# Experts chosen for twelve tiles beside the last output products, a first stage in a new order, and x1 kept in the weight ring

## The reference, cut to what matters

```python
def reference(x, c, w_ada, b_ada, ...):
    cond = jax.nn.silu(c)
    ada = (cond @ w_ada[l] + b_ada[l])[:, None, :]
    sh1, sc1, g1, sh2, sc2, g2 = jnp.split(ada, 6, axis=-1)
    h = rms_norm(x, norm1_gain[l]) * (1.0 + sc1) + sh1
    mix, v_first = token_mixer(h, ...)        # h @ w_in, a short convolution, a recurrence by chunks, @ w_out
    x = x + g1 * mix
    h2 = rms_norm(x, norm2_gain[l]) * (1.0 + sc2) + sh2
    x = x + g2 * moe(h2, w_router, router_bias, w_expert_in[l], w_expert_out[l])
    return rms_norm(x, final_gain)

def moe(h, w_router, router_bias, w_e_in, w_e_out):
    aff = jax.nn.sigmoid(hf @ w_router)
    sel = (aff + router_bias).reshape(t, N_GROUPS, EXPERTS_PER_GROUP)
    gscore = jnp.sum(lax.top_k(sel, TOP_K)[0], axis=-1)     # best group of 8, then the top 2 of its 4 experts
    gsel = jnp.argmax(gscore, axis=-1)
    ...
    # rows sorted by expert, each expert padded to blocks of 128 rows
    yb = lax.map(expert_block, (buf.reshape(n_blocks, M_BLK, d), blk_e))
    ye = yb.reshape(n_rows, d)[dest] * wts...
    return jnp.zeros_like(hf).at[tok].add(ye)
```

## Time and profile before

| | us |
|---|---|
| three runs | 4644.1, 4650.66, 4652.82 (median 4650.66) |
| the profiled execution | 4651.68 |
| its span in the trace | 4649.9 |
| first stage | 152.7 |
| last output product to the list of rows (`IDX`) | 3361.6 to 3451.6, 90 |
| last stage | 4556.3 to 4649.9, 93.6 |
| busy: PE, DVE, ACT, POOL | 4245.8 (91%), 1599.6 (34%), 1310.1 (28%), 321.6 (7%) |

### The profile page before, as it was taken

One profiled execution on the slowest core, in us unless ns is written; L12 is line 12 of the kernel. 1 busy time (PEld: TensorE's weight loads), 2 busy tenths in 40 slices (PEclk: granted clock), 3 DMA queues, 4 the chain that ended last, 5 costly groups with the idle time before them and its releaser, 6 DMA issues.

```text
span 4649.9 us, 91708 instructions
## 1 busy us (share of the span) xinstructions
PE 4245.8 (91%) x36691; PEld 2256.6 (49%) x36691; DVE 1599.6 (34%) x3167; ACT 1310.1 (28%) x2960; POOL 321.6 (7%) x422
## 2 busy tenths in 40 slices
PE   6999999999999999999999999989949999999991
PEld 4455555555555555555555555555524444444440
DVE  3333433443334333434433443432241111111115
ACT  4123333333333333333333333333301111111115
POOL 0000100010001000000100010000000000000004
PEclk8999999999999999999999999999959999999995
DMA  8101000100100100100100100024349999999998
GB/s 313 52 8 36 23 11 22 36 9 16 41 13 9 48 8 13 46 11 8 50 11 8 40 19 11 6 83 151 112 161 411 411 411 411 411 411 411 411 411 328
DMA packets 251199, 628.36 MB, mean 135 GB/s; under 512 B 11602, under 2 KB 96820, under 8 KB 250804
## 3 DMA queue, kind: packets, MB, share of 16 engines
q1 hardware_dynamic: 232372, 555.52, 31.8%
q0 software_dynamic: 11520, 41.95, 2.3%
q10 hardware_dynamic: 6912, 25.17, 1.3%
HBM read 561.75 MB, written 60.84 MB: 134 GB/s over the span
## 4 chain that ended last, share of the span: by engine, by line
PE 86%; issue 5%; DVE 4%; DMA 2%; ACT 2%; SPq 1%; POOL 0%; DVEq 0%; POOLq 0%; ACTq 0%
PE bank L958 38%; PE bank L1295 9%; PE bank L1299 5%; PE bank L1172 5%; PE bank L1325 5%; PE duo L1083 4%; PE bank L1329 2%; PE duo L1072 2%; PE duo L1070 1%; DMA yb<-y_s,dix 1%; PE duo L1276 1%; ACT xs L1361 1%; PE bank L1015 1%; PE duo L895 1%; PE bank L999 1%
## 5 line engine op out<-in xcount | busy, mean ns | idle before, releaser
L958 PE MATMUL bank<-hT,w 128*128 (+1 forms) x4096 | 1790.3, 594 | 0.0
L958 PEld LDWEIGHTS bank<-hT,w 128*128 128x128 f32 x4096 | 777.1, 190 | 993.4 <-issue 993.4
L1295 PE MATMUL bank<-W,xT 128*128 128x512 f32 x1024 | 446.5, 594 | 2.2 <-DVE xT L2200 1.5
L1361 ACT ACT_TABLE_LOAD x268 | 343.8, 1283 | 21.0 <-DVE ub L1919 14.3
L1295 PEld LDWEIGHTS bank<-W,xT 128*128 128x128 f32 x1024 | 192.7, 191 | 233.3 <-issue 233.3
L2206 DVE TENSOR_TENSOR gsig<-bank,gsig 128x512 f32<-128x512 f32 x48 | 33.2, 692 | 672.8 <-ACT gsig L1361 672.8
L1299 PE MATMUL bank<-W,xT 128*64 128x512 f32 x1024 | 227.2, 598 | 18.0 <-issue 18.0
L723 POOL TENSOR_TENSOR Tm<-Tm,idents 128x512 f32<-128x512 f32 x32 | 40.5, 1265 | 2822.2 <-DVE Tm L1952 2822.2
L1172 PE MATMUL bank<-wo,mT 128*128 128x512 f32 x512 | 232.5, 600 | 0.0
L1325 PE MATMUL bank<-W,aT 128*128 128x512 f32 x512 | 225.1, 592 | 0.0
L1361 ACT ACTIVATE gsig<-bank 128x512 f32<-128x512 f32 x48 | 28.7, 597 | 657.8 <-PE bank L1295 423.3
(11 more groups left out here) (366 smaller groups left out, 5520.0 us busy)
## 6 DMA issues: line engine op xcount, KB each, us to landing
W<-in_w_expert_in_dram SPq DMA_DIRECT2D x128, 2048.0 KB, 25.5
W<-in_w_expert_out_dram SPq DMA_DIRECT2D x64, 2048.0 KB, 25.4
w<-in_w_in_dram SPq DMA_DIRECT2D x64, 512.0 KB, 3.9
adaw<-in_w_ada_dram SPq DMA_DIRECT2D x12, 2048.0 KB, 12.7
y_s<-ysb ACTq DMA_DIRECT2D x48, 512.0 KB, 6.7
xt<-in_x_dram SPq DMA_DIRECT2D x16, 512.0 KB, 9.1
WAc<-rank_s SPq DMA_DIRECT2D x32, 256.0 KB, 3.3
GDc<-rank_s SPq DMA_DIRECT2D x32, 256.0 KB, 3.3
```

The lines of the kernel that those rows point to most:

```text
L958: ins = mm(PJ[j % 2][:, :], w[:, j, k, :], hT[:, k, ds(group(i) * G, G)], start=k == 0, stop=k == KT - 1)
L1295: ins = mm(GU[half][:, :], xT[:, slot, kk_, :], ring_rows(parts[0])[:, k, cols], start=kk_ == 0, stop=kk_ == KT - 1)
L1361: return nc.scalar.activation(o, i, f, **kw)
```

## The change

It has three parts.

*First stage.* The four pieces of `rows2` are loaded first, by SP, and the fourteen pieces of `rows1` are loaded from ACT's queue; `cond` is made before the mask constants are finished. On all engines the order of a group becomes: `rank(g)`, then the transposes and evacuation of group g + 1, then two parts of `ada`. ACT evacuates group 0 before it takes the norm of group 1, and evacuates group g + 1 between its two halves of `rank`. On SP the save of group 0 and the loads of x group 3 and of parts 6 and 7 come before the eight column blocks, where the column blocks came before the first save.

*Choice of experts.* The chain is written as functions of a part: part 0 is tiles 0 to 11, part 1 tiles 12 to 15. Part 0 is worked through on DVE between the residuals and evacuations of the last four tiles, ACT takes its sigmoid then (`affinity(0)`), and PE its counts (`ranks(0)`). Part 1 follows after the last logits, on a quarter of the elements. The block table is compared on 128 partitions (one `tensor_scalar` and one reduction of 128 x 64) and turned into a row by two small products on PE (`M0`, `M1`). The step L2125 moves behind `blk`. The tiles of the stage are laid elsewhere in SBUF so that this may overlap.

*Last stage.* x1 is loaded as four pieces of 2 MB, each into a slot of `W1`, as soon as PE is through with that slot, while the last experts are computed; the buffer `x8` is gone. All gathers' indices are copied once. ACT takes root and exponent for two tiles at a time, and DVE writes the outputs of a pair after the additions of the next pair. The loops over tiles are written out.

```diff
+        pw = ExitStack()
+        W1 = sb(pw, "W1", [P, 4, KT * DE])
         p7 = ExitStack()
-        W1 = sb(p7, "W1", [P, 4, KT * DE])
...
+        X_SLOTS = (0, 1, 4, 5)
+
+        def x_rows8(n):
+
+            return W1[:, n // NF, n % NF * D:n % NF * D + D]
...
+            sp.dma_start(rows2[10:18, :], rows_of(io["c"])).then_inc(S["rows2_in"], 16)
+            sp.dma_start(rows2[0:8, :], rows_of(io["norm2_gain"])).then_inc(S["rows2_in"], 16)
+            sp.dma_start(rows2[8:10, :], mu[24:26, :]).then_inc(S["rows2_in"], 16)
+            sp.dma_start(rows2[18:66, :], rows_of(io["b_ada"])).then_inc(S["rows2_in"], 16)
...
-            load_x(3)
             load_ups(0)
             load_gate(0)
+            save_rank(0)
+            load_x(3)
+            for n in ADA_OF[1]:
+                load_ada(n)
+            sp.wait_ge(S["rank_saved"], 32)
+            sp.dma_start(WAc[:, :], rank_s[0, :, 0:G]).then_inc(S["wa_in"], 16)
+            sp.dma_start(GDc[:, :], rank_s[1, :, 0:G]).then_inc(S["gd_in"], 16)
             for j in range(8):
                 load_col(j, 0)
-            for g in range(NG):
+            for g in range(1, NG):
                 save_rank(g)
-                if g == 0:
-                    sp.wait_ge(S["rank_saved"], 32)
-                    sp.dma_start(WAc[:, :], rank_s[0, :, 0:G]).then_inc(S["wa_in"], 16)
-                    sp.dma_start(GDc[:, :], rank_s[1, :, 0:G]).then_inc(S["gd_in"], 16)
                 if g + 1 < NG:
                     for n in ADA_OF[g + 1]:
                         load_ada(n)
...
-            def load8(n, s):
-                if not new8(n):
-                    sp.wait_ge(S["x2_ready"], n - NF + 1)
-                sp.dma_start(x8[:, s], x1_s[ds(n * P, P), :]).then_inc(x_rows_in[s], 16)
+            def load8(g):
+                ring_free(NB // 6, X_SLOTS[g])
+                sp.dma_start(W1[:, g, :].rearrange("p (t d) -> p t d", d=D),
+                             x1_s[g * NF * P:(g + 1) * NF * P, :].rearrange("(t p) d -> p t d", p=P))\
+                    .then_inc(x_rows_in[g], 16)
...
-            for s in range(2):
-                sp.wait_ge(SL["y_out"][s], 16 * ((NBLK + 1 - s) // 2))
-            for s in range(NF):
-                load8(s, s)
-            with sp.Fori(1, NTILE // NF) as h:
...
+            for g in range(NTILE // NF):
+                load8(g)
+            for n in range(NTILE):
+                store8(n, n % NF)
...
             for g in range(NG):
+                rank(g)
                 if g + 1 < NG:
-                    if g:
-                        for n in ADA_OF[g - 1]:
-                            ada(n)
-                        for n in ADA_OF[g - 1]:
-                            ada_columns(n)
                     transpose_x(g + 1)
-                if g == NG - 1:
-                    for n in ADA_OF[2]:
-                        ada(n)
-                    for n in ADA_OF[2]:
-                        ada_columns(n)
-                rank(g)
-            for n in ADA_OF[3]:
-                ada(n)
-            for n in ADA_OF[3]:
-                ada_columns(n)
+                for n in ADA_OF[g]:
+                    ada(n)
+                for n in ADA_OF[g]:
+                    ada_columns(n)
             pe.wait_ge(S["ada_col"], 12)
             tr(SA[0:48, 0:P], adaT[:, :], ident[:, :]).then_inc(S["ada_T"], 1)
...
+            def ranks(part):
+                cols = tile_cols(part)
+                pe.wait_ge(S["rank_mm"], 2 * part + 1)
+                mm(PJ[0][:, cols], sut[:, :], lg[6][:, cols], start=True, stop=True)
+                mm(PJ[1][:, cols], onesq[:, :], lg[6][:, cols], start=True, stop=True).then_inc(S["rank_mm"], 1)
+
+            pe.wait_ge(S["patterns"], 16)
             xn_T(NTILE - 2, 0)
+            ranks(0)
+            xn_T(NTILE - 1, 1)
             logits(NTILE - 2, 0)
-            xn_T(NTILE - 1, 1)
             logits(NTILE - 1, 1)
-
-
-            pe.wait_ge(S["rank_mm"], 1)
-            pe.wait_ge(S["patterns"], 17)
-            mm(PJ[0][:, :], sut[:, :], lg[6][:, :], start=True, stop=True)
-            mm(PJ[1][:, :], onesq[:, :], lg[6][:, :], start=True, stop=True).then_inc(S["rank_mm"], 1)
+            ranks(1)
+            pe.wait_ge(S["rank_mm"], 5)
+            mm(M0[0:1, 0:NB], bcol[:, 0:1], ident[:, 0:NB], start=True, stop=True)
+            mm(M1[0:1, 0:2 * NP], bcol[:, 1:2], pcol[:, :], start=True, stop=True).then_inc(S["rank_mm"], 1)
             for j in range(2):
...
-            norm_x(1)
             act.wait_ge(S["mod_ready"], 1)
             evac_x(0)
+            norm_x(1)
             for g in range(NG):
+                rank_scale(g, 0)
+                rank_out(g, 0)
+                rank_scale(g, 1)
                 if g + 1 < NG:
                     evac_x(g + 1)
+                rank_out(g, 1)
                 if g + 2 < NG:
                     norm_x(g + 2)
-                rank(g)
 
...
+            affinity(0)
+            for s in range(2):
+                evac5(NTILE - 4 + s, s)
+                copy_logits(NTILE - 4 + s)
+                norm2(NTILE - 2 + s, s)
             evac5(NTILE - 2, 0)
             evac5(NTILE - 1, 1)
-            act.wait_ge(S["logit_copied"], NTILE)
-            fn(aff[:, :], aff[:, :], ACT.Sigmoid).then_inc(S["aff_ready"], 1)
+            copy_logits(NTILE - 2)
+            copy_logits(NTILE - 1)
+            affinity(1)
...
+            def rstd8(n, s):
+
+                pair = slice(s, s + 2)
+                act.wait_ge(S["sumsq"], 2 * NTILE + n + 2)
+                fn(st8[:, pair, 1], st8[:, pair, 0], ACT.Ln, scale=1.0 / D, bias=epsc[:, 0:1]).then_inc(S["ln_done"], 1)
+                act.wait_ge(S["ln_done"], 2 * NTILE + n // 2 + 1)
                 if not new8(n):
-                    act.wait_ge(S["o_ready"], n - NF + 1)
-                fn(st8[:, s, 2:3], st8[:, s, 1:2], ACT.Exp, scale=-0.5).then_inc(S["rstd"], 1)
+                    act.wait_ge(S["o_ready"], n - NF + 2)
+                fn(st8[:, pair, 2], st8[:, pair, 1], ACT.Exp, scale=-0.5).then_inc(S["rstd"], 1)
 
             for s in range(2):
...
+            for n in range(0, NTILE, 2):
+                square8(n, n % NF)
+                square8(n + 1, n % NF + 1)
+                rstd8(n, n % NF)
...
+            evac5(NTILE - 4, 0)
+            groups(0)
+            residual(NTILE - 2, 0)
+            scale5(NTILE - 2, 0)
+            pick(0, 0)
+            evac5(NTILE - 3, 1)
+            pick(0, 1)
+            residual(NTILE - 1, 1)
+            scale5(NTILE - 1, 1)
             evac5(NTILE - 2, 0)
             evac5(NTILE - 1, 1)
-
-
-            dve.wait_ge(S["aff_ready"], 1)
-            dve.wait_ge(S["patterns"], 17)
+            link(TS(pcol[:, :], pidx[:, :], tid[:, 0:1], None, ALU.is_equal))
+            running(0)
+
+
+            groups(1)
...
+            pick(1, 0)
+            pick(1, 1)
...
+            running(1)
...
+            link(TS(bcmp[:, :, :], src[:, :, NE:], tid[:, 0:1], None, ALU.is_le))
+            RED(bcol[:, :], bcmp[:, :, :], AX.X, ALU.add).then_inc(S["rank_mm"], 1)
+            dve.wait_ge(S["rank_mm"], 6)
+            link(V.tensor_copy(bf[0:1, :], M0[0:1, 0:NB]))
+            link(V.tensor_copy(bp[0:1, :, :].rearrange("p g l -> p (g l)"), M1[0:1, 0:2 * NP]))
...
+            link(TT(rank[:, NE:], rank[:, NE:], tot[:, 0:RW - NE], ALU.add))
 
...
+            for n in range(0, NTILE, 2):
+                tile8(n, n % NF)
+                tile8(n + 1, n % NF + 1)
+                if n:
+                    out8(n - 2, (n - 2) % NF)
+                    out8(n - 1, (n - 1) % NF)
+            out8(NTILE - 2, NF - 2)
             out8(NTILE - 1, NF - 1)
```

337 lines of the change are left out of this document (159 added, 178 removed).

## The result

The changed kernel took 4600.54 us (median of four runs, 4594.88 to 4611.14) beside 4651.74 for the kernel before (four runs, 4644.1 to 4656.66). The ratio is 0.9894, with a 95% interval of 0.9869 to 0.9919: 49 us faster, give or take 12. The forecast was 4601. The profiled execution took 4605.25 us with a span of 4603.5, which is 46.4 us less than the span of before.

What follows compares the result with a forecast made beforehand. TensorE, with DMA full, bounds 3425 to 4556 us; the change works on three stretches where TensorE waits. 15.5 + 19.4 + 15.2 = 50.1 us off 4651.7 gives 4601.6, 1.0 less against the median: 4601, range 4588 to 4613.

Steps and rivals of the forecast that it cites:

- SP behind the column blocks: First stage: SP issues ada parts 8 and 9 late, so the end is about 5 us late: 137.3, gain 15.5.
- The estimate of 97 for SP's next save: First stage: after six megabytes (16 us) and 4.2 MB of columns (11 us), SP reaches its next save at about 97 us.
- The line between 32 and 512 elements: Choice, VectorE chain: from 182 ns at 32 elements and 692 at 512, 128 take 0.28 us and 384 take 0.56.
- Rival (d): Choice: part 0 is not covered, its 16.4 us lie on the path; gain 7, not 19.4; 4613 us; chance 0.05.
- the same 1105 us: Expert stage, a sign: the time from `IDX` to the last store of y stays at 1105 us.
- VectorE takes DMA's place, a little: Last stage: VectorE becomes the bound, its last addition at 4622 to 4624 against the last gather near 4621.
- The "82 us" in the list of signs: Last stage, a sign: the stage takes 82 us in place of 93.6.
- (a): First stage: SP is 5 us later still, and again before parts 10 and 11; gain 8, 4608 us; chance 0.13.
- (b): Last stage: x1's pieces delay the last weights or first gathers; the tail gains 8, 4608 us; chance 0.12.
- (c): First and last stage: all data on time, gains 20.4 and 20; 4591 us; chance 0.11.
- (e): Expert stage: TensorE starts at 1.2 GHz and stays there; 4691 us at four more such blocks; chance 0.02.
- (f): Last stage: DMA gives only 357 GB/s; gain 4 to 5 there, 4612 us in all; chance 0.05.

Runs made afterwards that it cites:

- The run with the save between: Changed kernel with the save of group 1 between the fourth and fifth column block of SP's list: 4604.0 us (one run), first stage 140.8 us.
- the run with x1 held: Changed kernel with all four loads of x1 held back until the last y has landed: 4631.6 us, ratio 0.9932 to the kernel before.
- the kernel with the columns at the end: Changed kernel with four of SP's column blocks behind ada parts 8 and 9, four behind the last save: 4607.1 us, ratio 0.9885 to the kernel before.

## Why the prediction was right

The forecast of 4601 and the median of 4600.54 are closer than the reasoning earns. By stages the traces gave 46.3 us where the sum had 50.1: last stage and choice gained what was forecast to within 1.2 us, the expert stage grew by 0.8 us more, and the middle, put at nothing, took 3.4. That the medians still agree to half a us is luck, beside an interval of 12 us either way and a middle that moves by 17 us in one and the same kernel.

**First stage, right to 0.1 us, with a term that I had mispriced.** `rank(0)` came at 41.4 instead of 43.2, since it started 3.8 us after ACT's evacuation began and not 5.0 or more. The 1.8 us put on it for coming out of a wait did not show (it took 13.97 us, the next one 13.91). The first `rank`s followed each other at 22.1 and 22.7 us, where the rows of before gave 21.7. The end hung on the loads all the same. The cause I named for the late end, SP behind the column blocks, and its result (part 9 landing near 112, the last `rank` at 115) were both what the trace shows: 112.0 and 114.6. The run with the save between confirms that the loads decide. Two things were missing. I had not seen that ACT needs the same save, since `rout` has one buffer a half; that wait, 7.59 us, lay beside the other, so it cost nothing more. And I priced the columns at 395 GB/s, 11 us; while they are in flight DMA moves 302, and they held SP for 19 us. The estimate of 97 for SP's next save does not follow from its terms: 65 + 16 + 13.4 is 94.4, and 94.0 was measured; the loads behind it were issued at 96.2. The hit to 0.1 us is thus partly luck: the repeats ended at 137.1 and 138.5.

**Choice, right in the chain and pessimistic about its start.** 46.7 us against the 46.6 that the sum had (67.5 less 19.4 and 1.5). The line between 32 and 512 elements gave the cost of 128 and 384 well: 0.29 and 0.56 us measured, 0.28 and 0.56 forecast; the block table took 1.4 for 1.7. The last residual was 2.65 us late (3.5 forecast), but the start was late by 0.2 and not 1.5. The gain up to `IDX` was 20.6 for 19.4. Rival (d), that twelve tiles' work is not covered, is out: it lies between 3327.5 and 3352.4, where VectorE had waited for ACT and TensorE before.

**Experts, right that nothing but the end moves.** The last store took 6.7 us for 2.6 as forecast, and the stage grew by 4.9 us for 4.1. Where the prediction said what would show it, it asked for "the same 1105 us", which forgot the 4.1 of its own sum; measured 1109.9.

**Last stage, right in size, half right in the bound.** From the last y to the end the sum had 4634.7 - 4560.4 = 74.3 us; measured 75.0. (The "82 us" in the list of signs was a slip against that sum, while "less than 10 us" of waiting fits only if counted from the stage's start: 9.8 of the 16.7.) "VectorE takes DMA's place, a little" holds as far as it goes: VectorE does not wait after its first addition, but the run with less work on it gained only 3 to 4 us, so the two are level. Its first addition came 9.8 us after the last y, where 7.1 were forecast; the tail was 10.1 for 11.

**Rivals.** Of (a), the further lateness before parts 10 and 11 did not occur here, but it is what came up as soon as parts 8 and 9 were made punctual. (b), x1 collides, is real in its mechanism (4.3 us by the run with x1 held), but its price, 4.1 us, was already in the forecast. (c) was excluded by part 9, (e) by TensorE's clock: 0.98 over the expert stage as before. (f), fewer bytes per us in a denser last stage, is out: 419 GB/s in the stretch from 4570 to 4590. The rule of some 358 GB/s per core (the Trainium skill, DMA: Bandwidth & Descriptors, Where 436 GB/s comes from) does not hold for this kernel on one core; the 425 that the same page has under Measured for 16 MB on a single core is the figure that these 419 agree with. What was not in any rival is the middle: the same kernel took 3175 to 3191 us there, a scatter larger than the error of the whole sum.

## What to carry to other kernels

Cut the trace at the stage borders and compare stage by stage: three gains of 13 to 21 us in 4650 repeat to 0.1 to 1.7 us in their own stretch, while an untouched part scatters by 17. When a queue serves loads and saves for several engines, moving one entry moves the wait to the next (part 9, then part 11, then the last save); follow it until the last late item has no transfer in flight ahead of it. A transfer pulled ahead of a byte-bound stage pays by its bytes, and costs what the last transfer before the stage loses beside it: here 14.3 us against 4.3.

## What the runs showed of the hardware

The eight column blocks have 512 bytes in a row (128 floats), where w_ada's parts have 2 KB. While they are in flight DMA counts as full but moves less. The stretch is of the changed kernel, with the columns of the view as in its first table:

```profile
82.00:97.00 15.00, 14.35 (x136) 7.71 (x125) 4.34 (x10) 9.89 (x16) 0.00 (x0) 1.00 1.19 302
```

302 GB/s at a share over 1.00, against 407 to 419 in stretches of the last stage. That the short rows are the cause was not tried. What such a transfer costs has to be read from a stretch in which its like is in flight, not from the best one.

And the issue is not free: eight of these blocks held SP for 13.4, 19.0 and 23.1 us in three orders. How long depends on what is in flight ahead of them. Four of them, first right behind two parts of `ada` (4.2 MB) and then with only a save ahead, in the kernel with the columns at the end:

```profile
86.19 15.94 SPq L482 DMA_DIRECT2D w<-in_w_in_dram  x4
...
125.78 5.05 SPq L482 DMA_DIRECT2D w<-in_w_in_dram  x4
```
